# Norms' factors as one product and ln/exp instead of columns, a root and a spread, in a kernel of two transformer blocks

## The chip, the cores and the metric

The kernel runs on one core of one Trainium2 chip. The metric is the device time of one execution in microseconds. Three runs were taken of the kernel before; their median counts.

## The reference

Two blocks run one after the other on x (512 tokens, width 1024), all in f32. The first: a SwiGLU ffn (width 2816), a mixer (windowed attention, and a long depthwise convolution with a layer norm, both gated), a second SwiGLU ffn, and a gated embedding `e`. The second: a mixer with pooling and a gated delta rule (4 heads of 128, chunks), cross attention to 256 memory tokens, and an ffn of width 4096 with a squared relu. Norms stand in front of nearly every stage:

```python
def rmsnorm_2(x, g):
    xf = x.astype(jnp.float32)
    y = xf * lax.rsqrt(jnp.mean(xf * xf, axis=-1, keepdims=True) + EPS)
    return (y * g.astype(jnp.float32)).astype(x.dtype)

def l2norm(x):
    return x * lax.rsqrt(jnp.sum(x * x, axis=-1, keepdims=True) + EPS)

# deltanet_mixer, cut
    qf = l2norm(qf.reshape(B, S, DN_HEADS, DN_HEAD_DIM))
    kf = l2norm(kf.reshape(B, S, DN_HEADS, DN_HEAD_DIM))
...
    o = o * lax.rsqrt(jnp.mean(o * o, axis=-1, keepdims=True) + EPS) * o_norm_g.astype(jnp.float32)
```

## The kernel before, in words

Everything is kept transposed: features on the 128 partitions, the 512 tokens along the free axis, eight tiles of that kind for a width of 1024. Each engine has its own program, written out by hand in the order in which it is to run: `tensor_program` (L303) for TensorE (PE), `scalar_program` (L1087) for ScalarE (ACT), `vector_program` (L1743) for VectorE (DVE) and `sync_program` for the DMA queue. They meet through named semaphore events (`tick` and `wait_ge`).

A gemm (L325) makes one tile of 128x512 from eight tiles of its input. Weight and input are each split in a high and a low part, so there are three matmuls a tile, 24 in all, one weight piece of 128x1024. The DMA queue brings the piece into one of three raw buffers, ACT copies it to `whi` (L1091, line of the copy L1098), DVE subtracts to get `wlo` (L1747, L1757). `after(key)` on ACT and DVE means: the weight pieces up to two behind this gemm. PE needs whi and wlo of a piece before it begins with it. `begun` (L351) is a gemm whose eight tiles can be issued in parts, with other work between them.

PE's results go to PSUM, eight banks of 128x512. `take` (L306) hands them out in a ring: it takes the bank at the front, puts it at the end again (unless it is pinned, in which case the program puts it back later by hand), and has PE wait until the key that held this bank last has been freed. The order of the `take`s thus fixes which event each product waits for.

A norm's factor is made in four steps. ACT squares the tiles and DVE sums them up in `acc` (for a head of 128 features one tile of squares in `scr` is enough). Then:

- `columns` (L371): four products of 128x128 by a column of ones give the sums of squares, one token per partition, four columns of 128 tokens.
- `deviation` (L1127) on ACT: the square root of these 4 columns (16 for the four key or query heads, `qk_deviation`, L1439), and `reciprocal` (L1793) on DVE.
- `spread` (L377) on PE: four products of the broadcast column and the identity turn them into a tile of 128x512 with the factor of each token on all partitions.
- `norm_R` (L1133) on ACT copies that tile to `Rt` in SBUF, or DVE reads it in PSUM.

The gemms before and after don't wait for it: the factor multiplies their results, when DVE takes them out of PSUM.

The stage of the second mixers (about 1245 to 1345 us): gemms cv4 to cv7 (keys), ab (decay and beta), cv0 to cv3 (queries), pi0 to pi3 (pooling), cv8 to cv11 (values). DVE multiplies each cv by Rt and does a convolution with four taps (L2201, L2204), ACT a Silu (L1429) and a square (L1437). Keys are heads 4 to 7, queries 0 to 3. PE takes the columns of keys 4 and 5 behind cv0, of 6 and 7 behind cv1 (a pinned bank), their spreads before pi0 and before pi1 (L630 to L633), those of the queries before chunks 0 and 1 (L674, L677). `bt` and `bt2` (L635) are banks for small columns, `bt` freed by ACT with the last Exp of `tc`. `unit_qk(i)` (L2207) on DVE multiplies a head by its factor and frees the factor's bank. It comes for the keys behind convolution 3 (L2348 to L2353), for queries 0 and 1 behind convolution 8 (L2366), for 2 and 3 behind convolution 9 (L2372). `chunk(h)` on PE (L656) makes four banks, bg, bb, kk and kq, and waits for key h before kk and for query h before kq.

In the rule that follows, `on_columns` (L825) and `on_spread` (L830) make the factor of each of four chunks of the output, read by DVE in `on_unit` (L2448).

Of the kernel before, what the change touches and what calls it, by code (L numbers as in the profile page):

```python
# [23 lines left out]
def shape_constants():  # L24

    p = np.arange(128)
    glob = np.zeros((128, 260), np.float32)
# [4 lines left out]
    glob[:, 258] = p >= 64  # L32
    c1 = np.zeros((128, 1152), np.float32)
# [73 lines left out]
def build(nc, io, book, plan):  # L107
# [10 lines left out]
    with ctx:  # L118
# [36 lines left out]
        cg = glob("cg", [128, 260])  # L155
# [147 lines left out]
        def tensor_program(pe):  # L303
# [108 lines left out]
            ffn("f1", "f1", Hh, Hl, "ffn1_wgu", "ffn1_wdown", True, [nothing, lambda: norm_columns("f1"), lambda: norm_R("f1")])  # L412
# [125 lines left out]
            for j in range(8):  # L538
                if j == 4:
                    ap4 = begun(("ap", 4), "attn_proj", 512, aoh, aol, "ao")  # L540
                    ap4(range(4))
                    spread("ln_mu", cols("mu", 4), ("mu",))
                    ap4(range(4, 8))
                else:
                    gemm(("ap", j), "attn_proj", 0, 8, [(128 * j, 128)], aoh, aol, "ao")
                if j == 3:
                    take(("cols", "ln"))
                    pe.wait_ge("conv_sum")
                    columns("ln", acc, ps(("cols", "ln")))
                if j == 7:  # L550
                    b = take(("cols", "lnv"))
                    pe.wait_ge("sum", "lnv", 7)
                    columns("lnv", acc, b)
            for j in range(3, 8):
                gate_b(j)
                if j == 3:
                    spread("ln_r", cols(("r", "lnv"), 4), ("r", "lnv"))
# [7 lines left out]
            for j in range(8):  # L565
                gemm(("pl", j), "ple_proj", 0, 2, [(128 * j, 128)], ph, pl, "p")
                if j == 2:
                    norm_columns("f2")
                if j == 4:
                    norm_R("f2")  # L570

            def e_columns():
                b = take(("cols", "e"))
                pe.wait_ge("sum", "e", 7)
                columns("e", acc, b)

            ffn("f2", "f2", Hh, Hl, "ffn2_wgu", "ffn2_wdown", True, [nothing, nothing, e_columns, nothing, lambda: spread("e", cols(("r", "e"), 4), ("r", "e"), pin=True)]
                + [nothing] * 9 + [lambda: ring.append(bank_of["R", "e"])])

            for j in range(8):
                gemm(("pg", j), "ple_gate_w", 0, 8, [(128 * j, 128)], H2h, H2l, "gate")
                if j == 0:
                    norm_columns("gate")
                if j == 1:
                    norm_R("gate")
# [17 lines left out]
            norm_columns("mix2")  # L605
            c4((7,))
            c5((7,))
            c6 = begun(("cv", 6), "w_in_2", 1280, Hh, Hl, "mix2")
            c6(range(4))
            norm_R("mix2")  # L610
            c6(range(4, 8))
# [10 lines left out]
            def k_spread(*tiles):  # L622
                for i in tiles:
                    spread(("qk", i), cols(("r", "k"), 16)[:, 4 * i - 16:4 * i - 12], ("r", "k"))

            def q_spread(*tiles):
                for i in tiles:
                    spread(("qk", i), cols(("r", "q"), 16)[:, 4 * i:4 * i + 4], ("r", "q"))

            k_spread(4, 5)  # L630
            other("pi", 0)
            k_spread(6, 7)
# [41 lines left out]
            q_spread(0, 1)  # L674
            chunk(0)
            conv4(9)
            q_spread(2, 3)  # L677
# [147 lines left out]
            def on_columns(c):  # L825
                b = take(("cols", ("on", c)))
                pe.wait_ge("on_sq", c)
                columns(("on", c), scr[c % 2], b)

            def on_spread(c):  # L830
                spread(("on", c), cols(("r", ("on", c)), 4), ("r", ("on", c)))

            for c in range(4):
                cur, v_ = St[c % 2], vn[c % 2]
                new = lambda h: u_[:, h, 0, :] if c == 0 else v_[:, h, :]
                if c:
# [6 lines left out]
                    on_columns(c - 1)  # L843
# [20 lines left out]
                if c:  # L864
                    on_spread(c - 1)
            first_half(2)
            on_columns(3)
            first_half(3)
            on_spread(3)
            first_half(4)  # L870
            for j in range(8):
                if j >= 5:
                    first_half(j)
                second_half(j)
# [89 lines left out]
            ffn("f3", "f3", Hh, Hl, "w_up_2", "w_down_2", False, [lambda: norm_columns("f3"), lambda: norm_R("f3")])  # L964
# [122 lines left out]
        def scalar_program(act):  # L1087
# [44 lines left out]

            def norm_R(name, prev, n=T):  # L1133
# [16 lines left out]
            def ffn(tag, name, prev, glu_, following):  # L1150
                for what, b in ffn_order(tag):
                    for f in range(f0[tag][b], f0[tag][b] + blocks[tag][b]) if what == "up" else ():
                        after((tag, "u", f))
                        if f == 0:
                            deviation(name, 4, 1.0 / D)
                            weights(ends[tag, "u", f] + 3)
                            norm_R(name, prev)
# [29 lines left out]
            def to_mix(j):  # L1187
                if j == 0:
                    act.wait_ge("gemm", last_up("f1"))
                    act.wait_ge("cols", "f1")  # L1190
# [137 lines left out]
            for j in range(8):  # L1328
                after(("ap", j))
                if j == 3:  # L1330
                    act.wait_ge("cols", "ln")
                    e.activation(cols("mu", 4), ps(("cols", "ln"))[:, 0:4], AF.Copy, scale=1.0 / D).then_inc(*act.tick("sd", ("mu",), ("free", ("cols", "ln"))))
# [4 lines left out]
            for j in range(3, 8):  # L1337
                after(("gb", j))
                if j == 3:
                    deviation("lnv", 4, 1.0 / D)  # L1340
# [10 lines left out]
            for j in range(8):  # L1351
# [5 lines left out]
                if j == 0:  # L1357
                    act.wait_ge("gemm", ("gb", 7))
                    act.wait_ge("cols", "lnv")
# [4 lines left out]
            for j in range(8):  # L1364
                after(("pl", j))
                if j == 3:
                    deviation("f2", 4, 1.0 / D)
                if j == 5:
                    norm_R("f2", "mix")
            for j in range(8):  # L1370
                act.wait_ge("eb", j)
                if j == 0:
                    act.wait_ge("cols", "f2")
                squares("e", j, eb[:, j, :])

            def glu_e(tag, f):
                if f == 1:
                    deviation("e", 4, 1.0 / D)
                glu(tag, f)

            def to_gate(j):
                if j == 0:
                    act.wait_ge("gemm", ("f2", "d", 1, 7))
                    act.wait_ge("cols", "e")
# [15 lines left out]
            def to_mix2(j):  # L1400
                act.wait_ge("x", "pg", j)
                if j == 0:
                    act.wait_ge("gemm", last_up("f2"))
                    act.wait_ge("cols", "gate")
# [6 lines left out]
            for j in range(8):  # L1411
                after(("pg", j))
                if j == 1:
                    deviation("gate", 4, 1.0 / D)
                    norm_R("gate", "f2")
# [15 lines left out]
            def qk_square(i):  # L1431
# [3 lines left out]
                elif i != 5:  # L1435
                    act.wait_ge("cols", ("qk", {7: 4, 0: 6, 1: 7, 2: 5, 3: 0}[i]))
                e.activation(scr[3 + i % 3][:, :], qkv[:, i, 4:516], AF.Square).then_inc(*act.tick("sq", ("qk_sq", i)))  # L1437

            def qk_deviation(key, last):  # L1439
                act.wait_ge("cols", ("qk", last))  # L1440
                e.activation(cols(("sd", key), 16), ps(("cols", key))[:, 0:16], AF.Sqrt, bias=epsc, scale=1.0).then_inc(
                    *act.tick("sd", ("sd", key), ("free", ("cols", key))))

            after(("cv", 4))
            deviation("mix2", 4, 1.0 / D)
            after(("cv", 5))
            norm_R("mix2", "gate")
# [29 lines left out]
            qk_deviation("k", 7)  # L1477
# [12 lines left out]
            qk_square(3)  # L1490
            after(("pi", 3))
            qk_deviation("q", 3)
# [78 lines left out]
            def on_square(c):  # L1571
                act.wait_ge("o", c)
                if c >= 2:
                    act.wait_ge("cols", ("on", c - 2))
# [1195 lines left out]
```

## Time and profile before

| | us |
|---|---|
| median of 3 runs | 2023.91 |
| lowest, highest | 2018.24, 2024.28 |
| the profiled execution | 2018.09 |
| its span, first to last instruction | 2016.3 |

The span is a little shorter than the time, since what lies around the first and last instruction isn't in it. Durations come from this one execution, whose time is near the lowest of the three runs. Busy time of PE is from modelled ends: matmuls overlap, so a matmul of 0.39 us is followed by the next after about 0.23 us. The distance between two starts is what a matmul costs in a row of them.

### The profile page before, as it was taken

The page shows a single profiled execution, that of the slowest core. Times are in us where ns is not written, and L with a number is a line of the kernel's source. Part 1 is how long each engine was busy: PE and PEld are TensorE (multiplying, and loading weights), DVE is VectorE, ACT ScalarE, POOL GpSimd, SP SyncE. Part 2 cuts the span into 40 slices and gives each one's busy share as a digit, 9 for nine tenths or more (in the row PEclk, how much of TensorE's full clock was granted, in tenths as well). Part 3 has the DMA queues.
Part 4 walks back from the last instruction along what each step waited for, and adds up shares of the span by engine and source line. Part 5 has one row for each costly group of instructions (what it writes and reads, how often), then busy time and mean ns, then how long its engine had stood idle before and what let it go on. Part 6 is the DMA issues. An engine that isn't in the chain of part 4 may idle for free. (4 is left out here: it accounts for less than half of the span.)

```text
span 2016.3 us, 26767 instructions
## 1 busy us (share of the span) xinstructions
PE 1985.0 (98%) x10554; PEld 1631.9 (81%) x10554; DVE 1210.0 (60%) x1714; ACT 809.3 (40%) x1232; POOL 16.2 (1%) x31
## 2 busy tenths in 40 slices
PE   8999999999999999999999999999999999999998
PEld 6888888887677788888888888877888888888887
DVE  6666565687889545654434367886464456544544
ACT  5444443433777253523322245541354432222222
POOL 0000000000000000000000000010000000000000
PEclk9999999999999999999999999999999999999999
DMA  6999886454333453333333233211143322223221
GB/s 238 300 301 294 291 292 238 173 177 141 120 116 121 172 188 111 110 103 95 94 97 96 88 101 94 84 43 35 38 135 117 109 90 94 94 95 105 94 95 72
DMA packets 80347, 274.84 MB, mean 136 GB/s; under 512 B 8928, under 2 KB 11488, under 8 KB 80224
## 3 DMA queue, kind: packets, MB, share of 16 engines
q1 hardware_dynamic: 79648, 272.36, 41.2%
q8 instruction: 84, 1.38, 0.3%
q10 hardware_dynamic: 576, 0.79, 0.1%
q14 instruction: 39, 0.32, 0.1%
HBM read 240.61 MB, written 32.51 MB: 135 GB/s over the span
## 5 line engine op out<-in xcount | busy, mean ns | idle before, releaser
L340 PE MATMUL ps<-Hh,whi 128*128 128x512 f32 x1448 | 571.8, 395 | 11.6 <-DVE Hl L1785 8.2
L344 PE MATMUL ps<-Hh,wlo 128*128 128x512 f32 x1448 | 564.6, 390 | 0.0
L341 PE MATMUL ps<-Hl,whi 128*128 128x512 f32 x1448 | 564.3, 390 | 0.0
L1098 ACT CAST whi<-raw 128x1024 fp32r<-128x1024 f32 (+3 forms) x352 | 350.0, 999 | 362.7 <-PE ps L344 339.8
L1757 DVE TENSOR_TENSOR wlo<-raw,whi 128x1024 fp32r<-128x1024 f32 (+3 forms) x294 | 338.4, 1157 | 171.0 <-ACT whi L1098 166.4
L340 PEld LDWEIGHTS ps<-Hh,whi 128*128 128x128 f32 x1448 | 272.3, 188 | 74.8 <-issue 12.8
L341 PEld LDWEIGHTS ps<-Hl,whi 128*128 128x128 f32 x1448 | 272.4, 188 | 57.0 <-issue 1.9
L344 PEld LDWEIGHTS ps<-Hh,wlo 128*128 128x128 f32 x1448 | 272.3, 188 | 57.1
L1873 DVE SCALAR_TENSOR_TENSOR cacc<-upad,gains,cacc 128x512 f32<-128x512 f32 x232 | 160.0, 743 | 0.7
L1823 DVE SCALAR_TENSOR_TENSOR x<-ps,x 128x512 f32<-128x512 f32 x79 | 54.6, 691 | 152.8 <-PE ps L344 152.8
L1799 DVE TENSOR_TENSOR scr<-ps,Rt 128x512 f32<-128x512 f32 x92 | 63.0, 686 | 56.5 <-PE ps L344 34.1
L344 PE MATMUL ps<-f3Ah,wlo 128*128 128x512 f32 x248 | 96.5, 389 | 0.0
L340 PE MATMUL ps<-f3Ah,whi 128*128 128x512 f32 x248 | 96.5, 389 | 0.0
L341 PE MATMUL ps<-f3Al,whi 128*128 128x512 f32 x248 | 96.5, 389 | 0.0
L1767 DVE TENSOR_TENSOR lo<-raw,hi 128x1024 fp32r<-128x1024 f32 x58 | 70.9, 1222 | 35.3 <-issue 18.0
L1110 ACT CAST hi<-raw 128x1024 fp32r<-128x1024 f32 x58 | 60.8, 1048 | 49.7 <-DVE lo L1767 25.8
L340 PE MATMUL ps<-f1Ah,whi 128*128 128x512 f32 x176 | 68.5, 389 | 0.0
L341 PE MATMUL ps<-f1Al,whi 128*128 128x512 f32 x176 | 68.5, 389 | 0.0
L344 PE MATMUL ps<-f1Ah,wlo 128*128 128x512 f32 x176 | 68.5, 389 | 0.0
L344 PE MATMUL ps<-f2Ah,wlo 128*128 128x512 f32 x176 | 68.5, 389 | 0.0
L340 PE MATMUL ps<-f2Ah,whi 128*128 128x512 f32 x176 | 68.5, 389 | 0.0
L341 PE MATMUL ps<-f2Al,whi 128*128 128x512 f32 x176 | 68.5, 389 | 0.0
(379 smaller groups left out, 2788.6 us busy)
## 6 DMA issues: line engine op xcount, KB each, us to landing
raw<-in_w SPq DMA_DIRECT2D x369, 512.0 KB, 4.1
low_parts<-lo SPq DMA_DIRECT2D x58, 512.0 KB, 4.4
wlo<-low_parts SPq DMA_DIRECT2D x58, 512.0 KB, 3.5
raw<-in_w SPq DMA_DIRECT2D x16, 384.0 KB, 3.1
raw<-in_w SPq DMA_DIRECT2D x17, 256.0 KB, 2.6
out<-y SPq DMA_DIRECT2D x8, 256.0 KB, 2.0
x<-in_x SPq DMA_DIRECT2D x5, 256.0 KB, 6.6
raw<-in_w SPq DMA_DIRECT2D x8, 128.0 KB, 2.0
```

What stands on the lines that cost most here:

```text
L340: e.matmul(out, h[:, kk, :], a, start=part != "last" and k + kk == 0, stop=False)
L341: e.matmul(out, h[:, kk, :], c, start=False, stop=False)
L344: ins = e.matmul(out, lo[:, kk, :], a, start=False, stop=done)
L1098: e.copy(whi[i % WS][:, 0:n], raw[i % RAWS][:, 0:n]).then_inc(*act.tick("whi", ("whi", i)))
L1110: e.copy(hi2[:, :], raw2[m % 2][:, :]).then_inc(*act.tick("hi2", ("hi2", m)))
L1757: e.tensor_tensor(wlo[i % WS][:, 0:n], src, h.bitcast(F32), SUB).then_inc(*dve.tick("wlo", ("wlo", i)))
L1767: e.tensor_tensor(lo2[m % 2][:, :], raw2[m % 2][:, :], hi2[:, :].bitcast(F32), SUB).then_inc(*dve.tick("lo2", ("lo2", m)))
L1799: return e.tensor_tensor(out, src, Rt[:, 0:n], MUL).then_inc(*dve.tick(kind, *names))
L1823: e.scalar_tensor_tensor(out=xj, in0=ps((tag, "d", b, j))[:, :], scalar=scale, in1=xj, op0=MUL, op1=ADD).then_inc(*dve.tick("x", ("x", tag ...
L1873: e.scalar_tensor_tensor(out=a if k < 30 else upad[:, j, 32:544], in0=src, scalar=wk, in1=a, op0=MUL, op1=ADD).then_inc(*dve.tick("conv", ...
```

## The change

For 20 factors (f1, the layer norm's mean and deviation, f2, e, gate, mix2, f3, eight key and query heads, four chunks of the output) the columns, the root, the reciprocal and the spread go. In their place:

- PE makes one product of 128x128 by 128x512 in f32, where the weights are a broadcast column of 1/1024 (new column 260 of `cg`) or of ones: each row of the result is the mean or the sum for each token. It comes where the columns came, and takes one bank.
- ACT makes Ln (with EPS as bias) and Exp with scale -0.5, in place in PSUM, or with the Exp into `Rt`. For the layer norm's mean nothing is left to do.
- DVE waits for the Exp instead of the spread. Its reciprocals go.

The factors of mix, xq, the memory and the last norm stay as they were. The banks of `ln_mu`, `ln_r` and `e` are pinned from the product on. Those of the heads and chunks aren't. One more first half (`first_half(5)`) goes in front of the second halves of `w_out_2`, and on DVE `unit_qk(2)` and `unit_qk(3)` move from behind convolution 9 to in front of `conv4_in(9)`.

```diff
+    glob[:, 260] = 1.0 / D
...
+            def mean_row(key, *up, src=acc, c=260, n=T, pin=False):
+                b = take(("R", key), pin)
+                pe.wait_ge("ld", "cg")
+                pe.wait_ge(*up)
+                e.matmul(b[:, 0:n], cg[:, c:c + 1].to_broadcast([128, 128]), src[:, 0:n], start=True, stop=True).then_inc(*pe.tick("spread", ("spread", key)))
+
+            def norm_row(name):
+                mean_row(name, "sum", name, 7)
...
                 if j == 3:
-                    take(("cols", "ln"))
-                    pe.wait_ge("conv_sum")
-                    columns("ln", acc, ps(("cols", "ln")))
+                    mean_row("ln_mu", "conv_sum", pin=True)
                 if j == 7:
-                    b = take(("cols", "lnv"))
-                    pe.wait_ge("sum", "lnv", 7)
-                    columns("lnv", acc, b)
+                    ring.append(bank_of["R", "ln_mu"])
+                    mean_row("ln_r", "sum", "lnv", 7, pin=True)
...
-                    norm_columns("f2")
-                if j == 4:
-                    norm_R("f2")
+                    norm_row("f2")
...
-            def qk_columns(*tiles):
+            def qk_rows(*tiles):
                 for i in tiles:
-                    pe.wait_ge("qk_sq", i)
-                    columns(("qk", i), scr[3 + i % 3], ps(("cols", "k" if i >= 4 else "q")), 4, 4 * (i % 4))
+                    mean_row(("qk", i), "qk_sq", i, src=scr[3 + i % 3], c=128)
...
             conv4(0)
-            take(("cols", "k"), pin=True)
-            qk_columns(4, 5)
+            qk_rows(4, 5)
             conv4(1)
-            qk_columns(6, 7)
-            ring.append(bank_of["cols", "k"])
+            qk_rows(6, 7)
             conv4(2)
             conv4(3)
...
-            k_spread(4, 5)
             other("pi", 0)
-            k_spread(6, 7)
             other("pi", 1)
...
-            take(("cols", "q"), pin=True)
-            qk_columns(0)
+            qk_rows(0)
             other("pi", 2)
-            qk_columns(1, 2)
+            qk_rows(1, 2)
             p3 = begun(("pi", 3), "w_in_2", 384, Hh, Hl, "mix2")
             p3(range(4))
-            qk_columns(3)
-            ring.append(bank_of["cols", "q"])
+            qk_rows(3)
             p3(range(4, 8))
...
             conv4(8)
-            q_spread(0, 1)
             chunk(0)
             conv4(9)
-            q_spread(2, 3)
             chunk(1)
...
-                    on_columns(c - 1)
+                    on_row(c - 1)
...
-                if c:
-                    on_spread(c - 1)
             first_half(2)
-            on_columns(3)
+            on_row(3)
             first_half(3)
-            on_spread(3)
             first_half(4)
+            first_half(5)
```

On ACT and DVE:

```diff
+            def root_row(key, scale=1.0):
+                b = ps(("R", key))[:, :]
+                act.wait_ge("spread", key)
+                e.activation(b, b, AF.Ln, bias=epsc, scale=scale).then_inc(*act.tick("sd", ("ln", key)))
+                act.wait_ge("ln", key)
+                e.activation(b, b, AF.Exp, scale=-0.5).then_inc(*act.tick("R", ("R", key)))
...
+            def qk_root(*tiles):
+                for i in tiles:
+                    b = ps(("R", ("qk", i)))[:, :]
+                    act.wait_ge("spread", ("qk", i))
+                    e.activation(b, b, AF.Ln, bias=epsc, scale=1.0).then_inc(*act.tick("sd", ("ln", ("qk", i))))
+                for i in tiles:
+                    b = ps(("R", ("qk", i)))[:, :]
+                    act.wait_ge("ln", ("qk", i))
+                    e.activation(b, b, AF.Exp, scale=-0.5).then_inc(*act.tick("R", ("R", ("qk", i))))
...
             qk_square(0)
-            qk_deviation("k", 7)
+            qk_root(4, 5, 6, 7)
             after(("cv", 3))
...
             qk_square(3)
+            qk_root(0, 1, 2)
             after(("pi", 3))
-            qk_deviation("q", 3)
+            qk_root(3)
             e.activation(tc[:, 48:80], ps("bt")[:, 0:32], AF.Exp).then_inc(*act.tick("tc", ("tc",), ("free", "bt")))
...
             chunk(0)
             after(("cv", 8))
+            unit_qk(2)
+            unit_qk(3)
             conv4_in(9)
             conv4(9)
-            unit_qk(2)
-            unit_qk(3)
             chunk(1)
```

## Rows read from the trace of the kernel before

**Rows 1.** The page: busy us, share of the span, instructions of PE.
```profile
PE 1985.0 (98%) x10554; PEld 1631.9 (81%) x10554; DVE 1210.0 (60%) x1714; ACT 809.3 (40%) x1232; POOL 16.2 (1%) x31
```

**Rows 2.** PE's waits: line, waited for, us in total, times, longest.
```profile
PE ps L374 <- DVE acc L1781: 1.5, 1, 1.5
...
PE ps L853 <- DVE vn L2489: 1.4, 1, 1.4
...
PE ps L382 <- DVE small L1795: 0.9, 1, 0.9
```

**Rows 3.** PE's timeline at mix2's columns and spread: start us, us, engine, line.
```profile
1244.94 0.95 PE L374 MATMUL ps<-cg,acc 128*128 128x1 f32 x8
...
1246.06 0.39 PE L364 MATMUL ps<-Hl,whi 128*128 128x512 f32 x1
...
1249.96 1.05 PE L382 MATMUL ps<-cg,small 128*128 128x128 f32 x8
...
1251.08 0.39 PE L364 MATMUL ps<-Hl,whi 128*128 128x512 f32 x1
```

**Rows 4.** PE's timeline at the rotary permutation, a f32 product of 512 columns.
```profile
434.30 1.10 PE L446 MATMUL ps<-scr,c 128*128 128x512 f32 x2
...
435.47 0.39 PE L341 MATMUL ps<-Hl,whi 128*128 128x512 f32 x1
435.70 0.39 PE L344 MATMUL ps<-Hh,wlo 128*128 128x512 f32 x1
```

**Rows 5.** ACT's timeline: the table loads before an Exp and before a Ln.
```profile
1272.39 1.28 ACT L1468 ACT_TABLE_LOAD   x1
...
1274.42 1.28 ACT L1471 ACT_TABLE_LOAD   x1
```

**Rows 6.** ACT's timeline: the keys' root (its table load) and the copy behind it.
```profile
1284.37 1.28 ACT L1441 ACT_TABLE_LOAD   x1
...
1285.83 1.04 ACT L1098 CAST whi<-raw 128x1024 fp32r<-128x1024 f32 x1
```

**Rows 7.** ACT's groups by line: us busy, mean ns, of two that read PSUM.
```profile
L1554 ACT ACTIVATE scr<-ps,gains 128x512 f32<-128x512 f32 x4 | 2.7, 687 | 0.4 <-PE ps L754 0.4
...
L1509 ACT ACTIVATE Tm<-ps 128x512 f32<-128x512 f32 x4 | 2.3, 578 | 0.0
```

**Rows 8.** DVE's timeline: pi1's weight subtraction, and the first two keys.
```profile
1290.20 1.22 DVE L1757 TENSOR_TENSOR wlo<-raw,whi 128x1024 fp32r<-128x1024 f32 x1
...
1301.88 1.27 DVE L2210 SCALAR_TENSOR_TENSOR qkv<-qkv,ps 128x512 f32<-128x512 f32 x2
```

**Rows 9.** PE's timeline: spread before pi0; first matmuls of pi1, cv8; query spreads; cv9; cv10.
```profile
1289.92 1.95 PE L382 MATMUL ps<-cg,small 128*128 128x128 f32 x16
...
1298.88 0.48 PE L340 MATMUL ps<-Hh,whi 128*128 128x512 f32 x1
...
1321.10 0.39 PE L340 MATMUL ps<-Hh,whi 128*128 128x512 f32 x1
...
1326.54 1.95 PE L382 MATMUL ps<-cg,small 128*128 128x128 f32 x16
...
1331.88 0.48 PE L340 MATMUL ps<-Hh,whi 128*128 128x512 f32 x1
...
1342.18 0.47 PE L340 MATMUL ps<-Hh,whi 128*128 128x512 f32 x1
```

**Rows 10.** DVE's timeline: the first two queries, behind convolution 8.
```profile
1330.23 1.28 DVE L2210 SCALAR_TENSOR_TENSOR qkv<-qkv,ps 128x512 f32<-128x512 f32 x2
```

**Rows 11.** PE's timeline behind the idle start of 8.2 us.
```profile
8.77 0.63 PE L341 MATMUL ps<-Hl,whi 128*128 128x512 f32 x1
9.20 0.63 PE L344 MATMUL ps<-Hh,wlo 128*128 128x512 f32 x1
```

**Rows 12.** Windows: from:to, length, then busy us (count) of PE, PEld, DVE, ACT, POOL, granted clock.
```profile
1384.00:1387.00 3.00, 1.03 (x25) 0.79 (x12) 0.59 (x1) 0.00 (x0) 0.00 (x0) 1.00 0.00 0
1387.00:1391.00 4.00, 4.00 (x43) 2.75 (x45) 3.10 (x5) 0.00 (x0) 0.00 (x0) 0.58 0.01 4
```

More of the change, by code:

```diff
@@ L567, in tensor_program @@
                 if j == 2:
-                    norm_columns("f2")
-                if j == 4:
-                    norm_R("f2")
[L572 to L578, printed above, removed]
+                    norm_row("f2")
+            ffn("f2", "f2", Hh, Hl, "ffn2_wgu", "ffn2_wdown", True, [nothing, nothing, lambda: mean_row("e", "sum", "e", 7, pin=True)]
+                + [nothing] * 11 + [lambda: ring.append(bank_of["R", "e"])])
             for j in range(8):
@@ L604, in tensor_program @@
             c5(range(7))
-            norm_columns("mix2")
+            norm_row("mix2")
             c4((7,))
             c5((7,))
[L608 to L611, printed above, removed]
+            conv4(6)
             conv4(7)
@@ L823, in second_half, with on_row @@
                 gemm(("w2", j), "w_out_2", 4, 4, [(128 * j, 128)], Ydh, Ydl, "yd", part="last")
[L825 to L831, printed above, removed]
+            def on_row(c):
+                mean_row(("on", c), "on_sq", c, src=scr[c % 2], c=128)
             for c in range(4):
@@ L1131, in deviation, with norm_row @@
                     *act.tick("sd", ("sd", key), ("free", ("cols", frees[0] if frees else key))))
+            def root_row(key, scale=1.0):
[4 more added lines that the diff above has]
+                e.activation(b, b, AF.Exp, scale=-0.5).then_inc(*act.tick("R", ("R", key)))
+            def norm_row(name, prev, n=T):
+                b = ps(("R", name))[:, 0:n]
+                act.wait_ge("spread", name)
+                e.activation(b, b, AF.Ln, bias=epsc, scale=1.0).then_inc(*act.tick("sd", ("ln", name)))
+                act.wait_ge("ln", name)
+                if prev:
+                    act.wait_ge("R_done", prev)
+                e.activation(Rt[:, 0:n], b, AF.Exp, scale=-0.5).then_inc(*act.tick("R", ("R", name), ("free", ("R", name))))
             def norm_R(name, prev, n=T):
@@ L1339, in scalar_program @@
                 if j == 3:
-                    deviation("lnv", 4, 1.0 / D)
+                    root_row("ln_r")
                 for i in range(3 * j - 12, min(3 * j - 9, 8)) if j > 3 else ():
@@ L1372, in scalar_program @@
                 if j == 0:
-                    act.wait_ge("cols", "f2")
+                    act.wait_ge("spread", "f2")
                 squares("e", j, eb[:, j, :])
@@ L1377, in glu_e @@
                 if f == 1:
-                    deviation("e", 4, 1.0 / D)
+                    root_row("e")
                 glu(tag, f)
@@ L1403, in to_mix2 @@
                     act.wait_ge("gemm", last_up("f2"))
-                    act.wait_ge("cols", "gate")
+                    act.wait_ge("spread", "gate")
                 norm_tile("mix2", "norm_mix_g_2", j, x[:, j, :], Hh)
@@ L1413, in scalar_program @@
                 if j == 1:
-                    deviation("gate", 4, 1.0 / D)
-                    norm_R("gate", "f2")
+                    norm_row("gate", "f2")
                     gate_sig(0)
@@ L1435, in qk_square @@
                 elif i != 5:
-                    act.wait_ge("cols", ("qk", {7: 4, 0: 6, 1: 7, 2: 5, 3: 0}[i]))
+                    act.wait_ge("spread", ("qk", {7: 4, 0: 6, 1: 7, 2: 5, 3: 0}[i]))
                 e.activation(scr[3 + i % 3][:, :], qkv[:, i, 4:516], AF.Square).then_inc(*act.tick("sq", ("qk_sq", i)))
[L1439 to L1442, printed above, removed]
+            def qk_root(*tiles):
[7 more added lines that the diff above has]
+                    e.activation(b, b, AF.Exp, scale=-0.5).then_inc(*act.tick("R", ("R", ("qk", i))))
             after(("cv", 4))
-            deviation("mix2", 4, 1.0 / D)
+            norm_row("mix2", "gate")
             after(("cv", 5))
-            norm_R("mix2", "gate")
             after(("cv", 6))
@@ L1573, in on_square @@
                 if c >= 2:
-                    act.wait_ge("cols", ("on", c - 2))
+                    act.wait_ge("spread", ("on", c - 2))
                 e.activation(scr[c % 2][:, :], ps(("o", c))[:, :], AF.Square).then_inc(*act.tick("sq", ("on_sq", c)))
             def on_high(c):
-                deviation(("on", c), 4, 1.0 / 128)
+                root_row(("on", c), 1.0 / 128)
             def yd_high(c):
@@ L1601, in scalar_program @@
                     act.wait_ge("gemm", ("po", 3))
-                    act.wait_ge("cols", "mix2")
+                    act.wait_ge("spread", "mix2")
                 norm_tile("xq", "norm_xattn_g_2", j, x[:, j, :], Hh)
@@ L1710, in to_last @@
                 if j == 0:
-                    act.wait_ge("cols", "f3")
+                    act.wait_ge("spread", "f3")
                 squares("last", j, x[:, j, :])
@@ L2121, in unit @@
                 names = [("e", j)] + ([("free", ("R", "e"))] if j == 7 else [])
-                dve.wait_ge("spread", "e")
+                dve.wait_ge("R", "e")
                 dve.wait_ge("sq", "e", 7)
@@ L2166, in vector_program @@
             after(("pg", 0))
-            reciprocal("gate", 4)
             after(("pg", 1))
@@ L2217, in vector_program @@
             after(("cv", 4))
-            reciprocal("mix2", 4)
             after(("cv", 5))
```

69 lines of the change are left out of this document (17 added, 52 removed).

## The prediction

> **What bounds the kernel.** I read the page first: TensorE (PE) is busy for 98% of the span [rows 1]. Then PE's waits: the longest one outside the start is 1.5 us, and only three touch the norms, 1.5 us before the columns of the layer norm, 0.9 us before its spread and 1.4 us behind the columns of the chunks' first norm [rows 2]. So a microsecond of PE work taken away is worth a microsecond, unless PE then stands before something that other engines don't deliver earlier. Those places I looked for in the timelines of PE, DVE and ACT around each norm, together with the order in which `take` hands out the eight PSUM banks.
>
> **What one swap is worth on PE.** Before, a norm of 512 tokens costs four column products and four spreading products. The columns begin at 1244.94 and the second matmul behind them at 1246.06; less one matmul of 0.23 us that makes 0.89 us. The spread, 1249.96 to 1251.08, makes 0.89 us too [rows 3]. The new product, 128x128 times 128x512 in f32, has a twin in the rotary permutation of L446: from 434.30 to 435.47 less 0.23 is 0.94 us [rows 4]. A swap saves 0.89 + 0.89 - 0.94 = 0.84 us.
>
> **The norms outside the second mixers.** f1, the layer norm's mean, e, gate and f3 stand between gemms that have their weights: 5 x 0.84 = 4.2 us. The row of each goes where its columns went, so nothing starts earlier on PE, and the root is ready 1 to 5 us earlier than the old spread. ACT pays for it with an Ln and an Exp of 512 columns in place of a root of 4 and a copy; it has over 5 us per weight piece there and 1 us of work for it, so I cost that at nothing (without the cover, about 3 us a norm). The layer norm's deviation saves 0.84 and the wait of 0.9 before its spread: 1.7 us; the 1.5 us before it stays, since it hangs on DVE's squares. The four chunks' norms save 4 x 0.84, less 0.3 us for squares that PE now meets a little earlier: 3.1 us; the first one's row lies in the shadow of the 1.4 us wait [rows 2]. f2 stands between `ple_proj` gemms of only 1.4 us each, and their weight copies on ACT now queue behind the whole root, some 2.5 us more: bounds 0.84 saved and 1 lost, I take 0.2 saved. Sum: 4.2 + 1.7 + 3.1 + 0.2 = 9.2 us saved.
>
> **The ACT side of a root.** Between the Exp at 1272.39 and the Ln at 1274.42 the trace shows a table load of 1.28 us each [rows 5]: the table that came for Exp did not hold Ln, although the Ln was two instructions away. I therefore take two loads for every Ln and Exp pair, one before each. The Trainium skill, "ScalarE: Activation LUTs", section on table sets, says that ln followed by exp needs one load, since one set holds both; no row here has that order. By that rule the sum falls by 4.3 us (second rival). Ln reads PSUM with a bias column: nearest row 0.69 us with one such operand; Exp 0.58 us without [rows 7]; back to back each hides 0.1.
>
> **Keys: where the bank order bites.** The rows of the keys now sit in their banks from the product until `unit_qk`, and are not pinned. Counting `take`s: R4, R5, cv1, R6, R7, cv2, cv3, pi0, and the ninth, pi1, gets the bank of R4. So PE can't begin pi1 before DVE has done `unit_qk(4)`, which stands behind `conv4(3)` at 1301.88 [rows 8]. Before, the spreads were in front of pi0 and pi1, and pi1 began at 1298.88 without a wait [rows 9].
> Now ACT. The root of keys 4 to 7 starts at 1284.37, and before, the weight copy behind it started at 1285.83 [rows 6]. New: two loads 2.57, four Ln 2.5, four Exp 2.1, 7.2 us together: the copy starts 1291.5, ends 1292.5, and DVE's subtraction of that piece, which began at 1290.20, begins 2.3 us later. From there ACT and DVE hand work to each other (subtraction, convolution 2, its Silu and square, the copy, the next subtraction, convolution 3) up to `unit_qk(4)` [rows 8], so it ends at 1301.88 + 0.64 + 2.3 = 1304.8. Everything here is 0.84 earlier by mix2's own swap: 1304.0. PE would be ready at 1289.92 [rows 9] - 0.84 + 5.45 = 1294.5. It stands for 9.5 us, and pi1 starts **5.1 us later than before**, with the 3.4 us of the keys' spreads already taken out.
>
> **Queries.** cv8 gets the bank of bt, which ACT frees with the Exp of `tc`, last behind the roots of 0, 1, 2 and then 3. From the end of pi2: row 2 is there after 1.95 us, its Ln 0.7, load 1.3, three Exp 1.5, weight copy 1.05, load 1.3, Ln 0.7, load 1.3, Exp 0.6, the `tc` Exp 0.2: 10.6 us. PE is there after 8.2 (two rows, pi3, row 3). Stall **2.4 us**; before, cv8 began at 1321.10 without one [rows 9].
>
> **Chunk 0.** Before: from the end of cv8 (1326.54 + 0.16) PE took 5.2 us to cv9 (1331.88) and 15.5 to cv10 (1342.18), of which 1.88 each time were query spreads, gone now [rows 9]. But `bb(0)` gets the bank of R0, kq(0) that of R1 and cv9 that of R2. DVE starts `unit_qk(0)` only behind convolution 8, 3.5 us after cv8's end, and ends 0.7 later (1330.23 and 0.64) [rows 10]. So PE stands 3.7 us before bb(0), then does bb, kk and kq to 7.0; DVE's four products of chunk 0 end at 8.8, its weight subtraction at 10.0, `unit_qk(2)`, which the diff moves there, at 10.65. cv9 starts at 10.75 in place of 5.2, and with a spread less cv10 at 19.2 in place of 15.5: **3.7 us later**. Behind that the order of banks is as before.
>
> **The clock.** After its idle start of 8.2 us PE's matmuls come 0.43 us apart in place of 0.23 for eight of them, that is the 1.2 GHz level [rows 11]; and in the stretch from 1387 the mean granted clock is 0.58, after PE had been busy for 1.03 of 3 us [rows 12]; at half rate such a stretch costs about 1.7 us. The stall before pi1 is longer than both; the two in chunk 0 (3.7 and 3.7 us) lie near the second. Bounds: one fall or three (1.7 to 5.1); I take two, 3.4 us.
>
> **Sum.** 5.1 + 2.4 + 3.7 + 3.4 - 9.2 = +5.4 us. The profiled execution took 2018.09 us (span 2016.3), so 2023.5 for its like; the median of the three runs, 2023.91, lies 5.8 above it, and set on that the forecast is **2029.3 us**. What a measurement can tell from no change is about 0.3%, 6.1 us; the forecast is just inside.
>
> **Rivals.**
> *PE's work is all that counts* (the waits for banks don't come, because DVE is there in time). Then the eight tiles save another 8 x 0.85 and mix2 0.84: 9.2 + 6.8 + 0.8 = 17 us, 2007 us. For it: PE at 98% and almost no waits. Against: `unit_qk(4)` at 1301.88 is simply later than 1294.5. Chance 0.12.
> *One table load per root.* The key root is 1.3 us shorter, the query root 2.6 to 3.9, which empties the 2.4 us stall, f2 keeps its 0.84: 5.4 - 1.3 - 2.4 - 0.6 = +1.1, 2025 us. Chance 0.18.
> *ACT's roots are longer than I make them*, which is slower. Place: the chains to `unit_qk(4)` and to `tc`; each microsecond added there is one added to pi1 and to cv8, with nothing beside it. It decides from 0.7 us more than forecast in both together. If each of the five loads on those chains took twice the 1.28 of the row, the sum would be 5.4 + 6.4 = +11.8, 2036 us. For it: both chains are tight and the roots work in place in PSUM, which no row shows; a third fall of the clock points the same way. Against: the loads of the trace show no time around their 1.28 us [rows 5]. The Trainium skill, same page, section on what the load costs, gives 2.66 us a switch with a drain; by the rows here the drain is not there. Chance 0.28.
> *The forecast itself*: 0.42, own range 2024 to 2033; a quarter of it lies above +6.1.
>
> **Numbers.** Faster: the first rival, 0.12. Slower: the third, 0.28, and a quarter of the forecast, 0.1: 0.38. Same: the rest, 0.5. The range leaves out the first rival and the far end of the third: 2014 (one load, the clock falling once, and the lower level of the runs, 2018, for the median) to 2038 (the third with a further fall).
>
> **What would show it.** PE: L374 and L382 down by 80 products each, 20 new products near 0.94 us; a wait of 8 to 10 us at pi1 released by DVE's `unit_qk`, one of 2 to 3 at cv8 released by ACT, two near 4 in chunk 0; a granted clock under 1 behind them. ACT: a load before each Ln and before each first Exp. Everything outside 1240 to 1345 shorter by about 9 us. I am wrong if pi1 begins without a wait, if Exp follows Ln without a load, or if the stages outside the second mixers don't shrink.

## The result, and the profile after

The changed kernel took 2024.55 us in the median of 12 runs, the kernel before 2019.10 in 12 on the same chips: ratio 1.0023 [1.0013, 1.0034], 0.13 to 0.34% slower. The profiled execution has a span of 2023.0 us against 2016.3, +6.7. The median of 2023.91 on which the forecast was set belongs to three runs; over twelve the kernel before lies 4.8 us lower. A few executions of the runs below took 4000 to 8700 us whatever the kernel, and no ratio has them.

The page and PE's waits of the changed kernel (in the second: line, waited for, us in total, times, longest), against [rows 1, 2]:

```profile
PE 1974.4 (98%) x10274; PEld 1607.6 (79%) x10274; DVE 1209.0 (60%) x1701; ACT 850.6 (42%) x1270; POOL 14.8 (1%) x31
```
```profile
PE ps L341 <- DVE qkv L2181: 12.7, 2, 9.3
...
PE ps L634 <- DVE qkv L2181: 3.2, 1, 3.2
PE ps L341 <- ACT small L1474: 2.2, 1, 2.2
```

PE has 280 fewer instructions and 10.6 us less busy time, although part of what is left ran at half rate. In exchange there are four waits of over 2 us that weren't there, all in the second mixers (the first line holds two of them). L2181 is `unit_qk`, L1474 the Exp of `tc`, L634 the product bb. PE's timeline shows what a stall looks like from inside (start, us, engine, line):

```profile
1288.27 0.39 PE L345 MATMUL ps<-Hh,wlo 128*128 128x512 f32 x1
1297.99 0.79 PE L341 MATMUL ps<-Hh,whi 128*128 128x512 f32 x1 [9.33 <-DVE qkv L2181]
1298.58 0.63 PE L342 MATMUL ps<-Hl,whi 128*128 128x512 f32 x1
1299.01 0.63 PE L345 MATMUL ps<-Hh,wlo 128*128 128x512 f32 x1
...
1323.96 0.50 PE L341 MATMUL ps<-Hh,whi 128*128 128x512 f32 x1 [2.16 <-ACT small L1474]
...
1335.57 2.07 PE L634 MATMUL ps<-rows,cg 4*128 4x512 f32 x2 [3.21 <-DVE qkv L2181]
1337.57 2.08 PE L639 MATMUL ps<-qkv 128*128 128x128 f32 x8
1339.44 1.91 PE L644 MATMUL ps<-qkv 128*128 128x128 f32 x8
1344.69 0.80 PE L341 MATMUL ps<-Hh,whi 128*128 128x512 f32 x1 [3.33 <-DVE qkv L2181]
```

pi1, cv8, bb(0) and cv9, in this order. The matmuls behind pi1's start come 0.43 us apart in place of 0.23, as behind the idle start [rows 11]: the granted clock is at its half level there, called half rate below. The keys' root on ACT, to be held against [rows 5, 6]:

```profile
1277.49 1.28 ACT L1419 ACT_TABLE_LOAD   x1
1278.79 2.39 ACT L1419 ACTIVATE ps<-ps,cg 128x512 f32<-128x512 f32 x4
1281.20 1.28 ACT L1423 ACT_TABLE_LOAD   x1
1282.49 2.05 ACT L1423 ACTIVATE ps<-ps 128x512 f32<-128x512 f32 x4
1284.41 1.07 ACT L1063 CAST whi<-raw 128x1024 fp32r<-128x1024 f32 x1
```

Two loads of 1.28 us, one before the Ln group and one before the Exp group, 6.9 us from the first load to the copy (7.2 forecast).

**Where the time went**, by the start of four pieces of PE work (in brackets what was added since the line above):

```
                     before    after     after - before
norm product mix2    1244.94   1238.99   -5.95
pi1                  1298.88   1297.99   -0.89   (+5.06 in this stretch)
cv8                  1321.10   1323.96   +2.86   (+3.75)
cv10                 1342.18   1355.28   +13.10  (+10.24)
end of the span      2016.3    2023.0    +6.7    (-6.4)
```

5.95 us are gained ahead of the second mixers, 19.05 lost between mix2 and cv10, 6.4 gained behind.

### The profile page after: what moved, and what is told of

Its sections match the earlier page's. It is cut to its first block and busy times, and to the rows that moved or that the text cites. A ratio compares the mean times of both kernels' runs of the same rounds, so it can differ in the third digit from the quotient of the medians.

```text
span 2023.0 us, 26230 instructions
## 1 busy us (share of the span) xinstructions
PE 1974.4 (98%) x10274; PEld 1607.6 (79%) x10274; DVE 1209.0 (60%) x1701; ACT 850.6 (42%) x1270; POOL 14.8 (1%) x31
## 5 line engine op out<-in xcount | busy, mean ns | idle before, releaser
L341 PE MATMUL ps<-Hh,whi 128*128 128x512 f32 x1456 | 579.6, 398 | 26.4 <-DVE qkv L2181 12.7
L1079 ACT CAST f3Ah<-scr 128x512 fp32r<-128x512 f32 x32 | 19.9, 621 | 122.7 <-DVE scr L2566 122.7
```

The lines of the kernel that those rows point to most:

```text
L341: e.matmul(out, h[:, kk, :], a, start=part != "last" and k + kk == 0, stop=False)
```

## The experiments

All ratios are to the kernel before, run on the same chip; one thousandth is 2.0 us. The changed kernel itself stands at 1.0023, +4.6 us by its ratio.

**The two halves of the change.** First, the change with keys and queries left as before, all other norms' rows kept (the reverse part of the diff):

```diff
-            def qk_rows(*tiles):
-                    mean_row(("qk", i), "qk_sq", i, src=scr[3 + i % 3], c=128)
+            def qk_columns(*tiles):
+                    pe.wait_ge("qk_sq", i)
+                    columns(("qk", i), scr[3 + i % 3], ps(("cols", "k" if i >= 4 else "q")), 4, 4 * (i % 4))
...
-            qk_root(4, 5, 6, 7)
+            qk_deviation("k", 7)
```

> The change without the part for keys and queries (they keep columns, one root for four heads, a reciprocal and spreads); all the other norms' rows stay. Theory: the other norms really save PE time, and only the banks of the keys' and queries' rows gave it away. At the product of mix2 the changed kernel was 5.95 us ahead; with mix2's own swap 0.8, the chunks' norms 3.1 and f3 0.8 the whole should be 10 to 11 us under the kernel before, ratio 0.9947, and the waits of 9.3, 3.2, 3.3 and 2.2 us in the second mixers should be gone. Rival (the lead is lost wherever PE next meets DVE or ACT, whatever the keys do): 3 to 6 us under it, ratio 0.997 to 0.9985, with new waits in the second mixers. Rival (the norms save nothing, the lead at mix2 is an accident of one profile): ratio 1.000.

Measured: 2006.05 us, ratio 0.9937 [0.9923, 0.9951], 12.7 us under the kernel before; span 2004.3. The longest wait for `unit_qk` that is left is 0.33 us. cv10 starts at 1335.24, 6.9 us earlier than before. The other norms' rows bring more than the 10 to 11 us expected.

Then the complement, the kernel before with only the keys' and queries' part of the diff (`mean_row`, `qk_rows`, `qk_root`, the moved order on DVE):

> The complement of the first experiment: only the keys' and queries' tiles are changed, all other norms stay with columns and spreads. Theory (two parts that do not touch each other): the changed kernel less what the other norms brought in the first experiment, 12.8 us, so 5.5 + 12.8 = 18 us over the kernel before, ratio 1.009. By the prediction's own terms it would be 5.4 + 9.2 + 0.8 = 15.4 us, ratio 1.0076. Rival (the lead of 6 us at mix2 made the stalls of the second mixers longer, since ACT and DVE do not come earlier by as much): 12 us or less, ratio 1.006 or less.

Measured: 2037.35 us, ratio 1.0085 [1.0070, 1.0099], +17.2 us. Three of its waits are those of the changed kernel to a hundredth (9.33, 2.16, 3.21), the fourth is 3.21 in place of 3.33, although everything comes 5 to 7.5 us later there:

```profile
PE ps L341 <- DVE qkv L2228: 12.5, 2, 9.3
...
PE ps L656 <- DVE qkv L2228: 3.2, 1, 3.2
PE ps L341 <- ACT small L1511: 2.2, 1, 2.2
```

-12.7 + 17.2 = +4.5, and the whole change measured +4.6: within the intervals (about 3 us either way for each part) the parts add. The small net result is the difference of two clear effects.

**The banks.** The same change, with the scaling of the keys moved on DVE to where their roots are ready:

```diff
+            for i in (4, 5, 6, 7):
+                unit_qk(i)
             after(("cv", 3))
             conv4_in(2)
             conv4(2)
...
-            unit_qk(4)
-            unit_qk(5)
             pool_in(0)
             after(("pi", 1))
-            unit_qk(6)
-            unit_qk(7)
```

> The whole change, but DVE scales the keys' four heads right behind their root, in a stretch where it stood 2.2 us for ACT, and not behind the convolutions of heads 2 and 3. Nothing else moves. Theory (pi1 waits only for the bank, its weights are there): the 9.3 us stall goes, and the half-rate stretch of 7 us behind it, worth 3 to 3.5 us; 12 to 13 us under the changed kernel, ratio to the kernel before 0.996 to 0.997. Rival (the bank is only the last of several, the chain through ACT's root to the convolutions would hold PE a little later, at pi2 or at the queries' rows): 3 to 7 us under the changed kernel, ratio 0.999 to 1.001, with a new wait between 1289 and 1318. Rival (the clock costs nothing): 9.3 us under it.

Measured: ratio 0.9973 [0.9964, 0.9983], 2014.87 us. The same kernel once more, for a profile that can be read:

> The same kernel as the one with the keys scaled early, whose profiled execution was disturbed (4340 us), so that its clock could not be read; it came out 9.7 us under the changed kernel where 12 to 13 were expected. Theory: pi1 starts right behind pi0 near 1288.5, the half rate behind the old stall is gone, but the block of small products between pi1 and pi2 now brings a fall of its own (as in the kernel with both reorderings), 1.6 us, and chunk 0 keeps its 3.2 and 3.3 us stalls; span near 2012.5, ratio 0.997. Rival (the gain is smaller because a new wait of 2 to 3 us stands between 1289 and 1318): the wait is in PE's waits, pi2 or the queries' rows start late.

Measured: ratio 0.9967 [0.9954, 0.9980], 2014.23 us, span 2011.5. pi0 and pi1 follow each other without a wait, and the other three stalls (2.16, 3.21, 3.21) stand as they were. cv10 starts at 1342.67, 12.6 us before that of the changed kernel; 0.5 of them were there at mix2's product already, 9.5 come in up to pi1, the rest is half rate and 0.1 of a stall. The fall of the clock that I expected behind the small products between pi1 and pi2 isn't there: pi2 took 5.87 us, and the granted clock is 1.00 from 1292 to 1304. So it was the bank that held pi1; no second wait stood behind it. Of the 12.6 us, 11.5 are left in the span.

Next, the queries, with the keys' stall left in place:

```diff
             qk_root(0, 1, 2)
+            e.activation(tc[:, 48:80], ps("bt")[:, 0:32], AF.Exp).then_inc(*act.tick("tc", ("tc",), ("free", "bt")))
             after(("pi", 3))
             qk_root(3)
-            e.activation(tc[:, 48:80], ps("bt")[:, 0:32], AF.Exp).then_inc(*act.tick("tc", ("tc",), ("free", "bt")))
...
             window(2)
+            for i in (0, 1, 2):
+                unit_qk(i)
             after(("pi", 3))
             pool_in(3)
             window(3)
+            unit_qk(3)
             conv4_in(8)
             conv4(8)
-            unit_qk(0)
-            unit_qk(1)
             chunk(0)
             after(("cv", 8))
-            unit_qk(2)
-            unit_qk(3)
```

> The whole change, but ACT takes the Exp of tc between the root of heads 0 to 2 and that of head 3, and DVE scales the queries 0 to 2 ahead of the weight subtraction behind pi2, and 3 ahead of convolution 8. The keys stay as in the changed kernel, with their stall of 9.3 us. Theory: the stalls of 2.2 us at cv8, 3.2 before bb(0) and 3.3 before cv9 go, 8.7 us, and with them the half rate from 1335 to 1349, worth some 5 us (chunk 0's twenty small products and most of cv9); 12 to 14 us under the changed kernel, ratio to the kernel before 0.996. Rival (chunk 0's own products on DVE or the weights of cv9 hold PE in place of the banks): 4 to 8 us under it, with a wait of 2 us or more left in chunk 0.

Measured: 2009.40 us, ratio 0.9950 [0.9937, 0.9963], 14.7 us under the changed kernel. Only the first of the `unit_qk` waits is left, the one at cv8 is gone too, and between bb(0) and cv10 PE stands for nothing; cv10 starts at 1338.47.

Both together:

> Both reorderings together. Theory (two separate stalls and their half-rate stretches): the gains add, 25 us under the changed kernel, near 1999 us, ratio to the kernel before 0.990, and that is the first rival of the prediction (PE's work is all that counts, 17 us) plus a little clock. Rival (with the keys' stall gone PE reaches the queries' part 9 us earlier and ACT's four table loads and roots there become the bound): 15 to 20 us under the changed kernel, ratio 0.993 to 0.995, with a wait of ACT between pi2 and cv8.

Measured: 2001.23 us, ratio 0.9909 [0.9895, 0.9923], 23 us under the changed kernel and 18 under the one before; span 1998.7. The longest of PE's waits outside the start, among those named with another engine, is now the one that was there before:

```profile
PE ps L391 <- DVE acc L1762: 1.5, 1, 1.5
PE ps L367 <- DVE wlo L1738: 1.5, 1, 1.5
PE ps L820 <- DVE vn L2454: 1.3, 1, 1.3
```

ACT does not become the bound. 3 us are missing against the sum of the two gains (11.3 + 14.7 = 26). The intervals are about 3 us either way, so these 3 are not clear of noise; in the profiles, half of them is a fall of the clock behind pi1 that neither of the two has. The windows, from:to, length, busy of each engine, granted clock third from the end:

```profile
1292.00:1296.00 4.00, 4.00 (x35) 3.36 (x33) 3.07 (x4) 0.74 (x1) 0.00 (x0) 1.00 0.22 46
1296.00:1300.00 4.00, 4.00 (x10) 2.48 (x10) 2.85 (x4) 2.42 (x5) 0.00 (x0) 0.57 0.23 91
```

The fall comes behind the 24 four-column products of bt and bt2. So, on top of this kernel, they were put into pi2's gemm, six behind every second tile:

```diff
+            qk_rows(0)
+            p2 = begun(("pi", 2), "w_in_2", 256, Hh, Hl, "mix2")
             for b in range(4):
+                p2((2 * b, 2 * b + 1))
...
-            qk_rows(0)
-            other("pi", 2)
```

> The kernel with both reorderings (keys and queries scaled early), and in it the 24 four-column products of bt and bt2 are no longer one block of 1.9 us between pi1 and pi2 but six at a time within pi2's gemm. In the kernel with both reorderings the granted clock fell to 0.57 right behind that block and pi2 took 7.1 us in place of 5.6. Theory (a block of tiny matmuls counts as idleness for the clock): no fall there, 1.5 us under that kernel, ratio to the kernel before 0.990. Rival (the fall comes from elsewhere): the same time, 0.9909.

Measured: 1998.71 us, ratio 0.9890 [0.9875, 0.9906], 22 us under the kernel before: the best of all. The windows of the same stretch:

```profile
1296.00:1300.00 4.00, 4.00 (x25) 3.14 (x24) 2.86 (x4) 1.57 (x2) 0.00 (x0) 1.00 0.19 75
1300.00:1304.00 4.00, 4.00 (x23) 2.67 (x22) 3.83 (x9) 0.95 (x3) 0.00 (x0) 1.00 0.35 131
```

The clock stays at 1.00; but the intervals of the two kernels overlap, another fall of the former kernel (0.70 and 0.88 at 1356 to 1364, in the rule's stage) is missing in this one too, and the same block of small products ran without a fall in the kernel before, in the first experiment and in the one with the keys early. That the block causes falls is not shown.

**ACT's share.** The roots of keys and queries with an Exp in the place of the Ln, so that no load stands between the two. This kernel leaves the logarithm out, so it divides no length out of keys and queries:

```diff
-                    e.activation(b, b, AF.Ln, bias=epsc, scale=1.0).then_inc(*act.tick("sd", ("ln", ("qk", i))))
+                    e.activation(b, b, AF.Exp, bias=epsc, scale=0.001).then_inc(*act.tick("sd", ("ln", ("qk", i))))
...
-                    e.activation(b, b, AF.Exp, scale=-0.5).then_inc(*act.tick("R", ("R", ("qk", i))))
+                    e.activation(b, b, AF.Exp, scale=-5.0).then_inc(*act.tick("R", ("R", ("qk", i))))
```

> The changed kernel with the logarithm in the keys' and queries' roots replaced by an Exp of the same shape with the same operands, scale 0.001, and the second Exp's scale -5.0: keys and queries are scaled by nearly the same constant, their length is not divided out. What it saves is only table loads: the second of the keys' root and three of the four of the queries' roots. Theory (each microsecond of ACT on these chains is one of PE, until the wait is used up): pi1 1.3 us earlier with a stall of 8.0 in place of 9.3; the stall of 2.2 at cv8 gone, and the half rate of cv8 with it (1.7 us): 5 us under the changed kernel, ratio to the kernel before 0.9998. Rival (DVE's convolutions set unit_qk(4), the loads lie beside them): nothing at pi1, 2 to 4 us in all.

Measured: 2019.00 us, ratio 0.9997 [0.9988, 1.0007], 5.2 us under the changed kernel. The row of pi1's start:

```profile
1296.45 0.79 PE L341 MATMUL ps<-Hh,whi 128*128 128x512 f32 x1 [7.97 <-DVE qkv L2181]
```

The stall is 1.36 us shorter for a load of 1.28 us, and the one at cv8 is gone with its half rate. So the chain from the keys' root over copy, subtraction and convolutions to `unit_qk(4)` is tight. It is also about what the second rival of the prediction (one load per root, +1.1 us) would have given: as fast as before.

**The clock's share.** The changed kernel, with matmuls that nobody reads in the four stalls:

```diff
+            def filler(n, prev):
+                pe.wait_ge("free", prev)
+                for _ in range(n):
+                    e.matmul(ps(prev)[:, :], Hh[:, 1, 0:128], Hh[:, 0, :], start=True, stop=True)
...
+            filler(39, ("cv", 1))
             other("pi", 1)
...
+            filler(8, "bt2")
             conv4(8)
             chunk(0)
+            filler(18, ("pi", 3))
             conv4(9)
```

and 13 more ahead of bb(0).

> The changed kernel with matmuls that nobody reads in PE's four stalls: 39 of 0.23 us ahead of pi1, 8 ahead of cv8, 13 ahead of bb(0), 18 ahead of cv9, into banks that are free. PE begins the real work at the same moment as before, but has not stood idle. Theory (the clock falls because PE stood, and the fall costs 1.7 us in pi1, 1.7 in cv8, 3.3 in chunk 0's small products and 2.2 in cv9): granted clock 1.0 from 1288 to 1350, 8 to 9 us under the changed kernel, ratio to the kernel before 0.998. Rival (the prediction's two falls of 1.7): 3.4 us under it, ratio 1.0006. Rival (the clock falls for another reason than PE's idleness): no gain, ratio 1.002 or more.

Measured: 2020.68 us, ratio 1.0003 [0.9994, 1.0012], 4 us under the changed kernel. PE begins pi1 at the same moment, and now at full rate:

```profile
1298.00 0.50 PE L341 MATMUL ps<-Hh,whi 128*128 128x512 f32 x1 [0.54 <-DVE qkv L2192]
1298.34 0.40 PE L342 MATMUL ps<-Hl,whi 128*128 128x512 f32 x1
1298.57 0.39 PE L345 MATMUL ps<-Hh,wlo 128*128 128x512 f32 x1
```

The same three windows, first of the changed kernel, then of this one:

```profile
1292.00:1296.00 4.00, 0.00 (x0) 0.00 (x0) 3.27 (x5) 0.54 (x1) 0.00 (x0) 0.50 0.27 49
1296.00:1300.00 4.00, 2.01 (x5) 1.63 (x6) 3.96 (x6) 1.56 (x2) 0.00 (x0) 0.50 0.20 82
...
1336.00:1340.00 4.00, 4.00 (x13) 2.50 (x13) 0.51 (x3) 0.00 (x0) 0.00 (x0) 0.50 0.00 0
```
```profile
1292.00:1296.00 4.00, 4.00 (x20) 3.30 (x19) 3.26 (x5) 0.55 (x1) 0.00 (x0) 1.00 0.24 47
1296.00:1300.00 4.00, 3.46 (x16) 2.54 (x15) 3.96 (x6) 1.57 (x2) 0.00 (x0) 1.00 0.22 88
...
1336.00:1340.00 4.00, 4.00 (x19) 3.25 (x19) 3.86 (x6) 0.00 (x0) 2.38 (x4) 1.00 0.15 16
```

From pi1 to cv8 PE takes 24.39 us in place of 25.97, from cv8 to cv10 25.48 in place of 31.32: half rate cost 1.6 + 5.8 = 7.4 us there. Behind cv10 the filled kernel loses 2.7 of them again (670.4 us to the end against 667.7). The clock does not account for these 2.7: the filled kernel has a half-rate stretch at 1392 to 1400 (0.71 and 0.87), the changed kernel a like one at 1404 to 1412 (0.90 and 0.68). PE's waits do. In the first stage behind the mixers, that of the rule, PE stands several times where the profile shows nothing that it waits for ("issue"). First the changed kernel, then the filled one:

```profile
PE ps L669 <- issue: 3.8, 3, 1.6
```
```profile
PE ps L680 <- issue: 3.1, 3, 1.3
PE ps L364 <- issue: 2.5, 1, 2.5
PE ps L768 <- issue: 1.0, 1, 1.0
```

That is 6.6 us against 3.8, 2.8 more. From the 1.33 us wait for vn behind them to the end, both kernels take 582.6 us. So these pauses account for the 2.7 us; what makes them no run shows. The expected 8 to 9 us came out as 7.4 on the spot and 4 in the time.

## Why the prediction was nearly right in size and wrong in what it called it

The forecast was +5.4 us; the ratio says +4.6 and the medians +5.45. The mechanism held: rows in unpinned banks, two loads for a root, four stalls where they were put. Two steps failed. The bound of 6.1 us for what a measurement can tell made "no change" of a forecast of +5.4, and twelve runs of each tell +0.23% from zero. And the clock, put at 3.4 us, cost 7.4; a surplus elsewhere hid that. Term by term:

**The swap on PE.** 0.94 us was forecast for a product: the one of mix2 stands between 1238.99 and the second matmul behind it at 1240.08, less 0.23 that is 0.86, so a swap saves 0.92, not 0.84.

```profile
1238.99 1.02 PE L391 MATMUL ps<-acc,cg 128*128 128x512 f32 x2
1239.45 0.79 PE L364 MATMUL ps<-Hh,whi 128*128 128x512 f32 x1
1240.08 0.39 PE L365 MATMUL ps<-Hl,whi 128*128 128x512 f32 x1
```

**Norms outside the second mixers.** 9.2 us forecast, and mix2's own 0.8: 10.0; measured alone 12.7 (9.9 to 15.5). Up to mix2 it is 5.95 for 5.3. f2's forecast came true: PE waits 0.64 us for ACT's copy at 822.16, and of the swap some 0.2 is left. Behind cv10 it is 6.4 for 3.9; 1.5 of the surplus is a fall of the clock that is not there any more (4 us times what is missing from a clock of 1.00; before: 0.62 at 1388 to 1392 and 0.58 at 1428 to 1432, 3.2 us lost; after: 0.90 and 0.68 at 1404 to 1412, 1.7 us). Another 0.8 are the pauses without a shown cause in the rule's stage, 4.6 us before and 3.8 after. Neither is a saving of the norms, and neither was forecast.

**Keys.** 9.5 us of stall and +5.1 forecast, 9.33 and +5.06 measured. **cv8.** 2.4 forecast; 2.16 of stall, and of the 3.75 us of this stretch 2.2 without the half rate. **Chunk 0.** 3.7 forecast; 10.24 less 5.84 of half rate is 4.4, and the two stalls (3.21 and 3.33) are where they were put. The count of `take`s held at each place, and the early scaling, together with the earlier Exp of `tc`, empties exactly these four waits: it was the banks.

**The clock: the term that failed.** The prediction gave it two falls of 1.7 us, 3.4 together, bounds 1.7 to 5.1. It was 7.4. I priced a fall as one short stretch at half rate. But behind the stall at bb(0) PE's own small products of chunk 0 run at half rate too (bb, kk and kq 5.8 us from start to end in place of 3.1), cv9 starts with a fresh stall behind it, and the stall of 2.16 at cv8, which I had not counted, cost another 1.6. All four stalls were followed by half rate: 1.6 us in pi1, 1.6 in cv8 (7.28 us against 5.69 in the filled kernel), 4.2 from there to cv10. The price of a fall in a gemm was right, their number and the small products were not.

**What hid it.** Between mix2 and cv10 19.05 us went where 14.6 were forecast (5.1 + 2.4 + 3.7 + 3.4), 4.45 more, 4.0 of it clock; 0.65 and 2.5 more than forecast were saved ahead of it and behind it: 4.45 - 0.65 - 2.5 = 1.3, which is 6.7 less 5.4 on the profiled executions. That the sum fits is luck: 4 us too few for the clock against 3.2 too few for the savings, of which 2.3 come from falls and pauses that just lie differently.

**The call "no change": the step that failed.** Half of the chance went to "same", within 0.3%, because 6.1 us was taken for what a measurement can tell. Twelve runs of each told +0.23% from zero with an interval of 0.1% either way. The prediction gives no row for this bound; the three runs that it had spread over 6.0 us (2018.24 to 2024.28), and the spread of single runs is not the error of a median of many. The sum itself, slower by 5.4, was the better answer. By the time itself, 2024.55 lies within 2014 to 2038, but the forecast of 2029.3 is 4.8 too high, as much as the three-run median was off.

**The rivals.** PE's work alone (2007) was wrong for the change as made, and near for it once the reads of the banks are moved: 2001. One load per root: the loads are there twice; the Trainium skill, "ScalarE: Activation LUTs", table sets, says that ln followed by exp needs one, and the rows at 1277.49 and 1281.20 show a load before each; the measurement decides. Longer roots: the keys' took 6.9 us and not more than the 7.2 forecast. The next ACTIVATE starts 0.02 us behind a 1.28 us load, and the second load 0.02 us behind the Ln before it. So the price of 2.66 us, which the Trainium skill, same page, gives in the section on what the load costs, isn't seen here.

## What to carry to other kernels

Where the eight PSUM banks go round in a ring, a result that now stays in its bank until another engine has used it can be a new wait for whoever comes eight `take`s later: count the ring, and look at what that reader stands behind in its own queue. Here the reader stood behind two convolutions it had no need to wait for, and moving eight of its calls and one Exp turned 0.23% slower into 0.9% faster. Price a stall of PE with the half rate behind it (of the 19 us lost here, 7.4 were clock), and read "no difference" from the error of the median, not from the spread of three runs.

## What the runs showed of the hardware that I had not expected

A stall of the same length did not always cost the same. The 2.16 us before cv8 were followed by half rate in the changed kernel (cv8 took 7.28 us, granted clock 0.66 from 1324 to 1328) and in the one with the keys early (7.17), but not in the kernel with the keys and queries alone:

```profile
1331.47 0.50 PE L341 MATMUL ps<-Hh,whi 128*128 128x512 f32 x1 [2.16 <-ACT small L1511]
1331.81 0.39 PE L342 MATMUL ps<-Hl,whi 128*128 128x512 f32 x1
1332.04 0.40 PE L345 MATMUL ps<-Hh,wlo 128*128 128x512 f32 x1
```

There cv8 took 5.67 us. And where it did fall, it could fall late: in the changed kernel the first five matmuls behind the stall come at full rate, most of them 0.23 apart, and 0.43 only from 1325.60 on:

```profile
1324.99 0.39 PE L342 MATMUL ps<-Hl,whi 128*128 128x512 f32 x1
1325.22 0.58 PE L345 MATMUL ps<-Hh,wlo 128*128 128x512 f32 x1
1325.60 0.63 PE L341 MATMUL ps<-Hh,whi 128*128 128x512 f32 x1
1326.03 0.63 PE L342 MATMUL ps<-Hl,whi 128*128 128x512 f32 x1
```

Falls in the rule's stage sit at different places (1388 and 1428 before, 1404 after, 1392 with fillers, none but in the last 10 us in the best). Each of the four named with a place begins within 2 us of the end of a pause of PE of 1.4 to 2.5 us, and for three of these pauses the profile gives no cause: 1.97 us up to 1386.11 and 1.41 up to 1428.07 before, 1.57 up to 1405.51 after, 2.47 up to 1392.51 with fillers. But a pause of 1.87 us up to 1377.51 in the kernel with two Exps had no fall behind it (granted clock 1.00 to 1384). In the changed kernel and the three with the reads moved early, the pauses stand before the same products each time, the last 2, 51 and 71 of a group of 128, with lengths from 0.93 to 1.85 us; where fillers are put in ahead, they stand elsewhere. So a fall's price can be read from a profile, but for a stall of 2 us its coming could not be forecast from the stall alone.
